# One level of Strassen's scheme in the input projection of a hybrid layer: seven block products, two phases of 1024 tokens

## The reference

```python
xn = _rmsnorm(x, g_pre)
u = xn @ w_in                      # (2112 tokens, 1024) @ (1024, 10256)
gq, gk, gv, gg, glr, dq, dk, dv, dg, ga, gb = jnp.split(u, cuts, axis=-1)
z = glr @ w_gla_lr + b_gla_lr      # 16 columns of u, the low-rank decay
o_a, s_new = _gla(q, k, v, log_a, gla_s0)          # recurrence in chunks
o_g, lse_g = _dilated_prompt(qg, kg, vg, dil, span)  # three windows, dil 1, 4, 16
o_g, lse_g, nbuf = _dilated_sample(qg, kg, vg, bufs[g], dil, span)
merged = sigmoid(ga) * y_a + sigmoid(gb) * y_b
h = x + _rmsnorm(merged @ w_out, g_post)
h = h + (pe @ w_ple_proj) * sigmoid(h @ w_ple_gate)
```

## Time and profile before

| what | value |
|---|---|
| median of 3 runs | 2802.43 us (2802.29 to 2804.70) |
| span of the profiled execution | 2799.7 us, 40,580 instructions |
| TensorE matmuls (PE) | 2769.4 us, 99% |
| TensorE weight loads (PEld) | 1453.6 us, 52% |
| VectorE (DVE) | 1077.3 us, 38% |
| ScalarE (ACT) | 861.5 us, 31% |
| GpSimd (POOL) | 360.3 us, 13% |
| DMA | 558 MB, 199 GB/s on average |
| mean granted TensorE clock | 0.998 of full speed |

### The profile page before, as it was taken

One profiled execution on the slowest core, in us unless ns is written; L12 is line 12 of the kernel. 1 busy time (PEld: TensorE's weight loads), 2 busy tenths in 40 slices (PEclk: granted clock), 3 DMA queues, 4 the chain that ended last, 5 costly groups with the idle time before them and its releaser, 6 DMA issues.

```text
span 2799.7 us, 40580 instructions
## 1 busy us (share of the span) xinstructions
PE 2769.4 (99%) x16108; PEld 1453.6 (52%) x16108; DVE 1077.3 (38%) x2401; ACT 861.5 (31%) x1728; POOL 360.3 (13%) x601
## 2 busy tenths in 40 slices
PE   8999999999999999999999999999999899999998
PEld 4444456555545665666555555555544344444444
DVE  6211134444333443344223333333322655555452
ACT  5111124444312222333123321111112544444441
POOL 2000011111311002120011113222100000000000
PEclk9999999999999999999999999999999999999999
DMA  9543464655577566584576789787646966556642
GB/s 283 134 168 132 147 208 152 214 177 207 190 253 286 187 195 213 185 273 152 179 278 208 257 234 301 239 249 252 216 152 224 277 172 174 148 149 180 164 112 58
DMA packets 326542, 558.35 MB, mean 199 GB/s; under 512 B 179114, under 2 KB 184305, under 8 KB 321874
## 3 DMA queue, kind: packets, MB, share of 16 engines
q1 hardware_dynamic: 268722, 290.57, 34.9%
q0 software_dynamic: 43376, 231.63, 25.3%
q10 hardware_dynamic: 14256, 33.56, 3.3%
HBM read 378.70 MB, written 236.79 MB: 220 GB/s over the span
## 4 chain that ended last, share of the span: by engine, by line
PE 96%; DMA 1%; SPq 1%; DVE 1%; ACT 0%; issue 0%; POOL 0%; DVEq 0%; POOLq 0%
PE out L2654 40%; PE out L2214 22%; PE out L2651 18%; PE out L1143 2%; PE out L1128 2%; PE out L2657 2%; PE out L1134 1%; PE out L615 1%; PE out L626 1%; PE out L625 1%; PE out L1429 1%; PE out L1389 1%; DMA mix_pe_in<-in_p_prompt 1%; SPq L356 1%; PE out L1117 1%; PE out L1402 0%
## 5 line engine op out<-in xcount | busy, mean ns | idle before, releaser
L2654 PE MATMUL out<-w_hi,xn_hi 128*128 128x512 f16 x1792 | 679.9, 379 | 1.0 <-DVE w_lo L2514 0.5
L2654 PE MATMUL out<-w_lo,xn_hi 128*128 128x512 f16 x1792 | 679.4, 379 | 0.0
L2654 PE MATMUL out<-w_hi,xn_lo 128*128 128x512 f16 x1792 | 679.4, 379 | 0.0
L2545 ACT ACTIVATE stage<-out 128x512 f32<-128x512 f32 (+1 forms) x170 | 99.4, 585 | 926.9 <-PE out L2654 613.2
L2592 DVE TENSOR_SCALAR stage<-out 128x512 f32<-128x512 f32 (+1 forms) x170 | 114.7, 675 | 645.0 <-PE out L2654 398.4
L2651 PE MATMUL out<-xn_hi,w_hi 128*128 128x512 f16 x768 | 291.3, 379 | 0.0
L2651 PE MATMUL out<-xn_hi,w_lo 128*128 128x512 f16 x768 | 291.1, 379 | 0.0
L2651 PE MATMUL out<-xn_lo,w_hi 128*128 128x512 f16 x768 | 291.1, 379 | 0.0
L2654 PEld LDWEIGHTS out<-w_hi,xn_lo 128*128 128x128 f16 x1792 | 175.4, 98 | 211.5 <-issue 0.3
L2654 PEld LDWEIGHTS out<-w_hi,xn_hi 128*128 128x128 f16 x1792 | 175.8, 98 | 192.6 <-issue 6.2
L2654 PEld LDWEIGHTS out<-w_lo,xn_hi 128*128 128x128 f16 x1792 | 175.4, 98 | 186.4 <-issue 0.3
(11 more groups left out here) (320 smaller groups left out, 3950.5 us busy)
## 6 DMA issues: line engine op xcount, KB each, us to landing
out<-in_cache_kv_w POOLq DMA_DIRECT2D x64, 1020.0 KB, 9.8
U<-stage SPq DMA_DIRECT2D x224, 256.0 KB, 4.6
raw<-in_w_in SPq DMA_DIRECT2D x78, 512.0 KB, 5.1
UT<-stage SPq DMA_DIRECT2D x96, 256.0 KB, 4.2
sw_kc<-in_cache_kv_w ACTq DMA_DIRECT2D x24, 1024.0 KB, 9.6
sw_vc<-in_cache_kv_w POOLq DMA_DIRECT2D x24, 1024.0 KB, 9.4
sw_rows<-U POOLq DMA_DIRECT2D x32, 512.0 KB, 7.8
out<-in_cache_kv_w POOLq DMA_DIRECT2D x16, 1008.0 KB, 8.0
```

The lines of the kernel that those rows point to most:

```text
L2545: move_out(act, m, lambda o, x: act.activation(o, x, ACT.Copy, scale=1.0 / W_SCALE))
L2654: last = pe.matmul(out[m % 3][:, :], x[:, k, at:at + P], y[:, k, :], start=first, stop=final)
```

## The change

The product xn @ w_in is done by the Winograd form of one level of Strassen's scheme. Tokens, inner dimension and columns are each halved; of the 2 x 2 x 2 block products seven remain, of sums of blocks:

- The tokens are taken in two phases of 1024, and each phase does all 20 column tiles (40 generations G in all). A phase has four pairs of token tiles (`PAIRS`): tile j of its upper 512 tokens and tile j of its lower ones. A pair is kept in SBUF in seven forms of 512 inner columns (`xf`, f16 high and low): three blocks of x itself and four sums, which GpSimd makes (`Inputs.sum`). Two pairs are transposed by TensorE, all others by DMA. The second phase's pairs are prepared during the first, stored in DRAM (`XB`) and loaded at the phase change (`load_pairs`).
- A column tile of weights is loaded in two pieces of 1 MB. VectorE makes four sums of 128 x 1024 in place (`first_sum`, `cut_lo`), and seven forms are cut in place of four pieces (ScalarE the high, VectorE the low part, 128 x 1024 each).
- A generation has two halves D (two pairs each), each with seven products. A product is 4 x 3 steps of 256 moving columns for each of its two positions, into one bank of 128 x 512.
- Products are combined as they leave PSUM: ScalarE copies P1, and VectorE does seven additions of 128 x 512 for the other six, each bank plus a staging buffer, the next waiting for the one before it.
- The samples are projected in the first phase only (`SAMPLE_STEP`), as before without the scheme.
- The slots are new: 17 per generation in the first phase (8 and 9 for its halves), 20 in the second, 740 in all. The recurrence runs in two runs of 8 steps (slots from 72, every 6; from 625, every 7), the samples' attention moves into the first phase (from 236), window attention into the second (from 409, 481, 547), the cutting of the later weights to 95 (every 4 slots). The low-rank product is done once per phase. The ring `sw_rows` has two buffers in place of three. The staging of window results goes by half heads.

The core of the diff:

```diff
-    RING = 8
-    FIRST = 4
...
+    RING = 6
+    BY_TENSOR = 2
...
+    def sum(self, pool, k):
+        ...
+        upper, lower = (self.tile(i) for i in self.tiles(k))
+        pool.tensor_tensor(s[:, 2, :], lower[:, :BANK], lower[:, BANK:], ALU.add).then_inc(self.summed, 1)
+        pool.tensor_tensor(s[:, 1, :], lower[:, :BANK], upper[:, :BANK], ALU.subtract).then_inc(self.summed, 1)
+        pool.wait_ge(self.summed, base + 1)
+        pool.tensor_tensor(s[:, 0, :], s[:, 2, :], upper[:, :BANK], ALU.subtract).then_inc(self.summed, 1)
+        pool.wait_ge(self.summed, base + 3)
+        pool.tensor_tensor(s[:, 3, :], upper[:, BANK:], s[:, 0, :], ALU.subtract).then_inc(self.summed, 1)
...
+    def turn_rows(self, sp, k):
+        ...
+        for part in range(2):
+            wide = 3 * BANK if k == self.SAMPLE else FORMS * BANK
+            ...
+            sp.dma_start_transpose(dst, src).then_inc(self.row_turned[s], 16)
...
+    def cut_lo(self, dve, G, f):
+        dve.wait_ge(self.hi_ready, FORMS * G + f + 1)
+        dve.scalar_tensor_tensor(out=self.w[1][f][:, :, :], in0=self.sources[f], scalar=W_SCALE, in1=self.w[0][f][:, :, :],
+                                 op0=ALU.mult, op1=ALU.subtract).then_inc(self.lo_ready, 1)
+        if f in (P1, P2, P7):
+            dve.wait_ge(self.lo_ready, FORMS * G + f + 1)
+        if f == P1:
+            dve.wait_ge(self.sum_ready, 4 * G + 1)
+            dve.tensor_tensor(self.sources[P6], self.sources[P1], self.sources[P7], ALU.subtract).then_inc(self.sum_ready, 1)
+        if f == P2:
+            dve.wait_ge(self.sum_ready, 4 * G + 2)
+            dve.tensor_tensor(self.sources[P4], self.sources[P2], self.sources[P6], ALU.subtract).then_inc(self.sum_ready, 1)
+        if f == P7:
+            dve.tensor_tensor(self.sources[P5], self.sources[P3], self.sources[P6], ALU.subtract).then_inc(self.sum_ready, 1)
...
+    def add(self, dve, D, f, us, out, other):
+        return dve.scalar_tensor_tensor(out=out, in0=self.shaped(D, self.product(D, f, us), us), scalar=1.0 / W_SCALE, in1=other,
+                                        op0=ALU.mult, op1=ALU.add)
...
+    def multiply(self, pe, G, d, f, us, step):
+        u, step = us[step // STEPS], step % STEPS
+        k, i = divmod(step, 3)
+        x, w = self.xf[(0, 0, 1)[i]], self.w[(0, 1, 0)[i]][f]
+        ...
+        if turned(G):
+            return pe.matmul(out.rearrange("p (a t) -> p a t", t=P), w[:, k, d * P:(d + 1) * P], x[:, 2 * u:2 * u + 2, f * HALF_K + k, :],
+                             start=start, stop=stop)
+        return pe.matmul(out, x[:, 2 * d + u, f * HALF_K + k, :], w[:, k, :], start=start, stop=stop)
...
-    RING = 3
+    RING = 2
...
+HI_AT = ((4, 6, 6, 7, 9, 9, 10), (2, 4, 5, 6, 8, 9, 10))
+LO_AT = ((5, 7, 7, 8, 10, 11, 12), (3, 5, 6, 7, 9, 10, 11))
```

More of the change, by code:

```diff
@@ new lines, in length, with part, ended @@
+def length(f, us):
+    return 2 * STEPS if f == SAMPLE_STEP else STEPS * len(us)
+def part(D, c):
+    order, parts = products(D), PARTS[D // (2 * COLUMN_TILES)][D % 2]
+    total, at, pieces = sum(length(*turn) for turn in order), 0, []
+    low, high = total * c // parts, total * (c + 1) // parts
+    for turn in order:
+        a, b = max(low - at, 0), min(high - at, length(*turn))
+        if a < b:
+            pieces.append((*turn, a, b))
+        at += length(*turn)
+    return pieces
+def ended(q):
+    G, d, c = place(q)
+    return [(f, us) for f, us, _, b in part(2 * G + d, c) if b == length(f, us)]
@@ L190, with columns, turned @@
-CUT_SLOT, CUT_PERIOD = 170, 10
+SHIFT_PAIRS = (range(3, 27), range(42, 62))
+CUT_SLOT, CUT_PERIOD = 95, 4
+def columns(G):
+    column = ORDERS[G // COLUMN_TILES][G % COLUMN_TILES]
+    return column + (LOWRANK if column >= W_LOWRANK else 0)
+def turned(G):
+    return ORDERS[G // COLUMN_TILES][G % COLUMN_TILES] in TURNED
 def wait(eng, sem, n):
@@ L247, in has @@
[L247 to L260, removed]
+                (self.rstd_ready, n), (self.scaled, n), (self.summed, self.sums_before(self.PREPS)), (self.turned, units), (self.hi_ready, units),
@@ L301, in turn @@
[L301 to L312, removed]
+    def sum(self, pool, k):
+        s, base = self.sums[k % 2], self.sums_before(k)
+        if k >= 2:
+            self.wait_used(pool, k - 2)
+        pool.wait_ge(self.scaled, self.tiles(k)[-1] + 1)
+        if k == self.SAMPLE:
+            x = self.tile(self.tiles(k)[0])
+            pool.tensor_tensor(s[:SAMPLES, 0, :], x[:, :BANK], x[:, BANK:], ALU.add).then_inc(self.summed, 1)
+            return
+        upper, lower = (self.tile(i) for i in self.tiles(k))
[5 more added lines that the diff above has]
+        pool.tensor_tensor(s[:, 3, :], upper[:, BANK:], s[:, 0, :], ALU.subtract).then_inc(self.summed, 1)
@@ new lines, in source, with turn @@
+    def source(self, k, f):
+        kind, *at = self.SOURCES[f]
+        if kind == "s":
+            return self.sums[k % 2][:, at[0], :]
+        return self.tile(self.tiles(k)[at[0]])[:, at[1] * BANK:(at[1] + 1) * BANK]
+    def turn(self, pe, k, f):
+        n = k * FORMS + f
+        bank = self.bank[n % len(self.bank)]
+        pe.wait_ge(self.scaled, self.tiles(k)[1] + 1)
+        if self.SOURCES[f][0] == "s":
+            pe.wait_ge(self.summed, self.sums_before(k + 1))
+        wait(pe, self.lo_ready, n + 1 - len(self.bank))
+        src = self.source(k, f)
+        for b in range(HALF_K):
+            last = pe.transpose(bank[:, b * P:(b + 1) * P], src[:, b * P:(b + 1) * P], self.identity[:, :])
+        last.then_inc(self.turned, 1)
@@ L528, in left, with done @@
         return [(signal, n) for signal in steps] + [(self.crossing_ready, 2 * n)]
[L530 to L532 removed]
+    def done(self, eng, phase):
+        n = (phase + 1) * self.run
         wait(eng, self.state_ready, n)
@@ L2370, in side_queue @@
+            for phase in range(PHASES):
+                prompt_gla.queue(q, slot - GLA_SLOTS[phase], phase)
             sample_gla.queue(q, slot - GLA_SAMPLE_SLOT)
@@ L2674, in _ @@
+                projection.tensor(pe, q)
+                for phase in range(PHASES):
+                    lowrank.tensor(pe, phase, q - LOWRANK_SLOTS[phase], inputs, projection)
+                for phase in range(PHASES):
+                    prompt_gla.tensor(pe, q - GLA_SLOTS[phase], phase)
                 for g in range(GROUPS):
```

1375 lines of the change are left out of this document (853 added, 522 removed).

## The result

The changed kernel takes 2932.26 us (median of 4 runs, 2919.54 to 2936.32) against 2803.56 for the kernel before, a ratio of 1.045 (95% interval 1.0428 to 1.0475). It is slower by 129 us where I had forecast 40 us less. Its profiled execution spans 2917.4 us at a mean granted TensorE clock of 0.966; before it was 2799.7 and 0.998. The four executions lie 17 us apart and the profiled one is the fastest of them, so against the median the gains of e3, e4 and e6 would be some 13 us larger than by span. Runs e3 to e9 and e12 are one execution each.

What follows compares the result with a forecast made beforehand. TensorE, busy 99% of the span, was taken as the bound. Terms -190 + 13 + 46 + 8 + 24 + 24 + 28 + 8 = -39 gave 2799.7 - 39 + 2.7 = 2763 us; forecast's own range 2715 to 2797, overall 2685 to 2855.

Steps and rivals of the forecast that it cites:

- The matmuls, -190: Projection on TensorE: 13,440 matmuls of 256 columns at 109.1 ns, 1466 us where 1657 was before; -190 us.
- Rival 3: Projection matmuls: a 128-wide load does not hide behind 256 columns, 120 ns each, +147, 2910 us; chance 0.04.
- rival 4: Projection matmuls: as issued they aren't 7/8 in columns, so TensorE's busy time would stay; chance 0.01.
- VectorE's load: VectorE's additions, cuts and weight sums: 22.9 us per generation, busy about 1800 us in all.
- waits of TensorE name VectorE: Sign in TensorE's waits: VectorE's additions and window copies named, some 120 us; under 40 clean, over 130 Rival 2.
- Recurrence and the cutter: Chunked recurrence, 16 steps: VectorE's cuts, sums and step preparation lose 4.2 us some 5.6 times; +24 us (0 to 60).
- Samples, +28: Sample attention, 8 x 15 slots: row loads wait with the ring at 2, plus dense stretches; +28 us (5 to 70).
- Windows, +24: Window attention, 207 slots: stalls where a cut, sum and addition give VectorE 4.2 us of work; +24 us (5 to 60).
- x of phase two, +8: Second phase's x prepared in phase one: VectorE work and SyncE transposes every 9 slots, 2 us a pair; +8 us.
- Start, +46: First generation: fourth pair turned at about 84 to 88 us, end at 106 instead of 59; +46 us.
- The clock: Sign of being wrong: TensorE's granted clock falls after the long waits and stays low; no size given.
- Rival 2: Side stages: VectorE becomes the bound, each engine waiting for the other in turn; +93, 2895 us; chance 0.28.

Runs made afterwards that it cites:

- e3: Changed kernel with the four weight sums and the additions of P4, P5 and P3 done on 16 columns only: 2851.18 us.
- e4: Changed kernel with the later weights cut for 2 of 30 slices only, the other 28 stores issued again from the same buffers: 2870.76 us.
- e6: Changed kernel with the cutter starting in slot 76 with a slice every 5 slots, not from 95 every 4: 2877.12 us.
- e9: On top of e6, GpSimd issues the key and value copies into the caches after window attention, in generations 34 to 36: 2854.15 us.
- e12: e10 with VectorE's work lightened as in e3 (weight sums and additions of P4, P5, P3 on 16 columns): 2731.69 us.
- e8: On top of e6, first sample's values loaded 8 slots before the samples' attention; turn of row scores and value product one slot later: 2840.06 us.
- e7: On top of e6, second phase's pairs every 14 slots, their x loaded 8 slots ahead, not 4, cutter's gains three slots later: 2864.91 us.
- e14: On top of e10, first generation's samples' product sixth in its half, second phase's pairs prepared from slots 22, 28, 40 and 56: 2788.83 us.
- e10: Changed kernel with the edits of e6, e7, e8 and e9 together: 2801.96 us, ratio to before 1.0002.

## Why the prediction was wrong

**The matmuls, -190: right.** 109.2 ns against 109.1, 13,440 of them. Rival 3 (the pace) and rival 4 (no saving) are out.

**VectorE's load: right in size, mostly wrong as a cause.** 1767 us against about 1800. But "waits of TensorE name VectorE" was my test for it, and that test can't tell work from waiting: the name is that of the last engine in a chain. e3 and e12 can: some 320 us of VectorE's work cost 68 and 81 us of span. It cost where I had put it in the recurrence and the samples, and not in the windows, where I gave 24 us to slots with 4.2 us of work in them.

**The step that failed** is the one on which every stage's sum rests: that a transfer is in by the time its slot comes, so that only the engines' own work in a slot counts. In the last line of the prediction ScalarE and stores are named as what I "gave nothing"; that is where it went. TensorE's waits name ScalarE for 43 us, and a store never: the stores stand one or two engines further back. By term:

- *Recurrence and the cutter (generations 4 to 13).* I had the cutter at "every 4 slots, not 10" and costed nothing but its instructions. It has a single output buffer, which is cut, stored by SyncE in a later slot, and landed 5.4 us (median of 17 stores from 560 to 760 us) to 11.6 us (the chain above) after that: with 2.3 us for the two cuts and up to a slot (2.3) until the issue, even the median comes to about 10 us, over the 9.2 of 4 slots. 44 us (e6).
- *Samples, +28.* I had seen the smaller ring and two waits of 2.7 us a sample, by the 7.8 us of the earlier trace rows. That row is a median, and it hid what mattered. The trace of before has three of its 32 loads behind the same values, 18.8 to 19.9 us under way, and no wait of VectorE came of them there. After the change it took 23, and with the flip in the same slot as the last row product the stage lost 30 us more (e8).
- *Windows, +24.* What was late was a store of half a head, 37 us under way where 8 slots (23 us) were given; the change had halved that time, and I hadn't costed the finer staging at all: 28 us (e9).
- *x of phase two, +8.* Generations 1 to 3 took 171 us, where my terms come to 134 (3 x 39.3, half of the low-rank product's 15.5, and the 8). Of the 37 beyond, e7 gave back 14 and e14 another 3; 151 remain, and the rest is open. The move of 13 us of transposes past the weights' loads was in my text, but only as work, not as the 16 us wait it makes for VectorE when the load is due right behind.
- *Start, +46.* 117 us for 106. The fourth pair was turned at 85.4 as forecast (84 to 88). I had left out that the samples' rows are turned after it: TensorE waited 7.21 us for them at 99, at the lower clock. With the product put three places later the generation ends at 107.5.
- *The clock.* I named it as what would prove me wrong and gave it no term. With what else lies in TensorE's busy time it is 70 us of the 295 in after and 44 in e14; by the clock's record at most 59 and 35. The long waits were paid for again behind their end.

**Rival 2** (2895) comes within 37 us of the measured time, and rival 3 (2910) within 22, but by chance: the pace of rival 3 wasn't there, and e3 refutes the reason of rival 2 in the main. VectorE was 61 to 68% busy in the side stages of after, where rival 2 had near 90%. Its point of decision (131 us of stalls outside the start) was passed by another road.

From 2932 the five repairs lead to 2789, 26 us above the forecast of 2763: e10 alone gives 130 us, the start 13. What the last 26 us are I haven't tested; generations 1 to 3 are still 17 us above my terms, and e14's waits that remain are spread over the additions (25.6 us), the recurrence (13.2) and the start.

## What to carry to other kernels

When a change tightens a hand-written order (shorter slots, smaller rings, a shorter period), list each buffer that a transfer must fill or free, and set the slots between issue and use against the landing time at the busiest point of that queue, with all that is queued ahead, not against the median row. In a wait table go on from the engine named to what that engine stood for: a late result of VectorE may be a store that nobody counted. And before an engine is held for too slow, take work from it and leave its waits: here 322 us of work were worth 68 to 81.

## What the runs showed of the hardware

After a wait of 6.71 us TensorE's matmuls started 0.21 us apart for 4.6 us, then 0.109 again: the wait cost a third more than its length. In stretches with such waits the granted clock was 0.73 (50 to 100 us), 0.80 (850 to 900) and 0.86 (1750 to 1800).

Transposing 3584 columns by DMA occupied SyncE's queue for 4.1 to 4.9 us each (I had 6.5, from the earlier trace rows); it is what stands behind it that pays.

VectorE and GpSimd hold each other up, both ways. After's rows, beside each other and apart:

```profile
24.75 1.22 DVE L693 TENSOR_TENSOR raw<-raw 128x1024 f32<-128x1024 f32 x1
...
30.13 2.17 DVE L695 TENSOR_TENSOR raw<-raw 128x1024 f32<-128x1024 f32 x1
...
31.18 2.25 POOL L439 TENSOR_TENSOR sums<-x 128x512 f32<-128x512 f32 x1
...
57.53 1.27 POOL L439 TENSOR_TENSOR sums<-x 128x512 f32<-128x512 f32 x1
```

The same 128x1024 subtraction took 2.17 us beside GpSimd's sums and 1.22 alone, and a sum 2.25 us for 1.27 where VectorE was reading one operand out of PSUM (L478). In the prediction I had set the Trainium skill (SBUF — State Buffer, section "SBUF: two separate sides") against the earlier trace rows and gone by the rows, by which only GpSimd waits; the page has a VectorE instruction with two SBUF inputs and a GpSimd one that reads SBUF shut each other out for the whole instruction. These rows agree with it, and I was wrong. It mattered little: the mean of the 40 sums at L695 is 1.27 us.
